# Gated-memory heads: weights in two buffers, differences on ScalarE, products one step behind the weights

## What is computed

```python
D = jnp.where(mask, bh[..., :, None] - bh[..., None, :] + igh[..., None, :], -jnp.inf)
m_t = jnp.maximum(D.max(-1), m_inter)
S = jnp.einsum('bthd,bshd->bhts', qc, kc) * jnp.exp(D - m_t[..., None])
...
h = num / jnp.swapaxes(jnp.maximum(jnp.abs(den), jnp.exp(-m_t)), 1, 2)[..., None]
```

## Time and profile before

| what | value |
|---|---|
| median of three runs | 2977.45 us (2977.14, 2977.45, 2989.36) |
| the profiled execution | 2978.73 us, of which the span from first to last instruction is 2977.0 us |
| gated-memory stage | from about 430 to 545 us of the span |
| PE busy over the span | 2599.6 us (87%) |
| DVE, ACT busy over the span | 848.3 us (28%), 426.1 us (14%) |

### The profile page before, as it was taken

How to read it: one execution, slowest core, us unless ns; L and a number is a source line. 1 busy time by engine, 2 the same in 40 slices (tenths; PEclk the granted TensorE clock), 3 DMA queues, 4 the chain that set the end, 5 groups by cost and what they waited for, 6 DMA issues and landing times.

```text
span 2977.0 us, 34023 instructions
## 1 busy us (share of the span) xinstructions
PE 2599.6 (87%) x13714; PEld 1463.5 (49%) x13714; DVE 848.3 (28%) x1782; ACT 426.1 (14%) x794; POOL 203.2 (7%) x267
## 2 busy tenths in 40 slices
PE   5998986899999997999899888888789988888886
PEld 3454555444444444444486444444377944444443
DVE  3145638510020045300133211111167651111111
ACT  1032211110010013200101100000123411000001
POOL 3122111110010010000010000000000010000000
PEclk8999998899999999999999999999989999999998
DMA  6676578245453543244644599999943066999997
GB/s 243 213 238 245 201 259 286 92 164 168 136 191 132 169 145 99 101 147 159 236 155 146 225 415 420 419 418 420 367 133 99 6 219 243 413 418 420 419 421 303
DMA packets 264855, 721.87 MB, mean 242 GB/s; under 512 B 15248, under 2 KB 149040, under 8 KB 210864
## 3 DMA queue, kind: packets, MB, share of 16 engines
q1 hardware_dynamic: 251232, 690.00, 61.2%
q0 software_dynamic: 13520, 30.41, 3.1%
HBM read 719.17 MB, written 1.18 MB: 242 GB/s over the span
## 4 chain that ended last, share of the span: by engine, by line
PE 67%; DMA 19%; DVE 8%; SPq 2%; issue 2%; ACT 2%; POOL 0%; DVEq 0%; ACTq 0%; POOLq 0%
PE ps L891 23%; DMA ring<-in_moe_w_up 16%; PE ps L1504 9%; PE ps L998 7%; PE ps L916 5%; PE ps L1100 4%; PE ps L1082 2%; SPq L556 2%; DMA ring<-in_ada_w 2%; PE ps L1608 2%; PE ps L1054 2%; PE ps L1494 2%; PE ps L927 1%; PE ps L1444 1%; PE ps L1274 1%
## 5 line engine op out<-in xcount | busy, mean ns | idle before, releaser
L891 PE MATMUL ps<-ring,hT 128*128 128x512 f32 x1632 | 720.6, 596 | 16.6 <-ACT hT L1734 12.5
L891 PEld LDWEIGHTS ps<-ring,hT 128*128 128x128 f32 x1632 | 307.1, 191 | 382.5 <-issue 363.7
L1504 PE MATMUL ps<-arena 128*32 128x512 f32 x1536 | 271.3, 689 | 80.4 <-DMA ring<-in_moe_w_up 71.8
L1504 PE MATMUL ps<-ring,arena 128*32 128x512 f32 x512 | 270.6, 690 | 0.0
L1494 PEld LDWEIGHTS ps<-arena,h 128*128 128x128 f32 x1024 | 248.4, 334 | 17.6 <-issue 14.1
L1494 PE MATMUL ps<-arena,h 128*128 128x128 f32 x1024 | 245.2, 399 | 5.3 <-issue 5.3
L998 PE MATMUL ps<-ring,arena 128*128 128x512 f32 x528 | 232.2, 593 | 2.4 <-ACT arena L1800 2.4
L1504 PEld LDWEIGHTS ps<-arena 128*32 128x32 f32 x1536 | 69.7, 123 | 255.4 <-issue 198.8
L2274 DVE SCALAR_TENSOR_TENSOR arena<-ps,arena 128x256 f32<-128x256 f32 x66 | 28.0, 424 | 578.8 <-ACT arena L1796 578.6
L916 PE MATMUL ps<-hT,ring 128*128 128x256 f32 x768 | 172.3, 387 | 2.5 <-ACT hT L1734 1.5
L998 PEld LDWEIGHTS ps<-ring,arena 128*128 128x128 f32 x528 | 100.1, 190 | 127.7 <-issue 127.7
(11 more groups left out here) (530 smaller groups left out, 2437.8 us busy)
## 6 DMA issues: line engine op xcount, KB each, us to landing
ring<-in_moe_w_down SPq DMA_DIRECT2D x128, 1024.0 KB, 17.7
ring<-in_ada_w SPq DMA_DIRECT2D x48, 2048.0 KB, 12.2
arena<-in_moe_w_gate SPq DMA_DIRECT2D x96, 1024.0 KB, 11.7
arena<-in_moe_w_up SPq DMA_DIRECT2D x96, 1024.0 KB, 9.8
ring<-in_ffn_w_in SPq DMA_DIRECT2D x66, 1024.0 KB, 8.9
ring<-in_ffn_w_out SPq DMA_DIRECT2D x33, 1024.0 KB, 5.0
ring<-in_moe_w_gate SPq DMA_DIRECT2D x32, 1024.0 KB, 15.7
ring<-in_moe_w_up SPq DMA_DIRECT2D x32, 1024.0 KB, 17.8
```

The lines of the kernel that those rows point to most:

```text
L891: m = pe.matmul(o3, lhsT_of(k), ring[:, a:a + 2, k * EH:(k + 1) * EH], start=start and k == 0, stop=stop and k == KC - 1)
L1504: m = pe.matmul(ps[a * CAP:(a + 1) * CAP, 6, :].rearrange("p (u c) -> p u c", u=2), x_slots[:, k, a * CAP:(a + 1) * CAP], slot_pair(gate_s ...
```

## The change

- `p_sb` becomes two buffers, one for each direction.
- The differences move from DVE to ACT: a Relu with scale 1 that reads the row of maxima from `ps`, with -e as bias per partition (the transposed column is copied with scale -1). ACT does the four of a step, then the four exp.
- `seen_by` gives the columns that a key block can be seen from: 512, 384, 256, 128 forwards and 512, 512, 128, 256 backwards, in place of 512, 512, 256, 256. Relu, exp and the product with the scores do only those.
- One masking instruction covers all four diagonal blocks (a strided view, `own_blocks`) in place of four.
- DVE's `weighted(i + 1)` stands in step `i` ahead of the wait for PE's products of step `i`; `weighted(0)` stands before the loop.
- Scores of key blocks 2 and 3 share bank 2; bank 3 is then used for the conditioning groups. PE does the row of maxima two steps ahead, and the next head's scores ahead of the products of an odd step.
- On DVE the order of a step is: (step 0: waits for the values and `out_g`), sums of squares, `ada_rows`, `weighted(i + 1)`, wait for the products, drain.

```diff
-        p_sb = A(4, NT)
+        p_sb = A(2, 4, NT)
...
+        def own_blocks(b):
+            at = p_at + b * 4 * NT
+            return arena[:, at:at + 4 * (NT + P)].rearrange("p (s n) -> p s n", s=4)[:, :, 0:P]
+        def seen_by(si, d):
+            return slice(si * P, NT) if d == 0 else slice(0 if si < 2 else SEQ, NT if si < 2 else (si + 1) * P)
+        def scores_of(si, cols):
+            return ps[:, si, cols] if si < 2 else ps[:, 2, slice(cols.start - SEQ * (3 - si), cols.stop - SEQ * (3 - si))]
...
+            row_max(0)
+            row_max(1)
+            head_scores(0)
+            pe.wait_ge(tp_evacuated, n.tp)
             for hd in range(MLSTM_HEADS):
                 for d in range(2):
                     i = 2 * hd + d
                     pe.wait_ge(sem("ada_rows_ready"), ada_next[0])
-                    if i >= 2:
-                        pe.wait_ge(sem("ml_weights"), 4 * (i - 1))
...
-                    ada_groups(ADA_B[i], 5 - d)
+                    ada_groups(ADA_B[i], 3)
...
-                    pe.wait_ge(sem("ml_weights"), 4 * (i + 1))
+                    pe.wait_ge(sem("ml_weights"), i + 1)
+                    if i + 2 < 2 * MLSTM_HEADS:
+                        row_max(i + 2)
+                    if d == 1 and hd + 1 < MLSTM_HEADS:
+                        head_scores(hd + 1)
                     if i >= 1:
                         pe.wait_ge(sem("ml_out_read"), i)
...
             for i in range(8):
+                act.wait_ge(sem("ml_max"), i + 1)
+                if i >= 2:
+                    act.wait_ge(sem("ml_out"), i - 1)
                 for si in range(4):
-                    k = 4 * i + si
-                    act.wait_ge(sem("ml_gap"), k + 1)
-                    w = p_sb[:, si, (0 if si < 2 else SEQ):NT]
-                    tell(nc.scalar.activation(w, w, ACT.Exp, scale=-1.0), sem("ml_exp"))
+                    nc.scalar.activation(p_sb[:, d, si, seen_by(si, d)], ps[:, 4 + d, seen_by(si, d)], ACT.Relu,
+                                         bias=colsT[:, 0, si, row:row + 1]).then_inc(sem("ml_gap"), 1)
+                for si in range(4):
+                    act.wait_ge(sem("ml_gap"), 4 * i + si + 1)
+                    w = p_sb[:, d, si, seen_by(si, d)]
+                    nc.scalar.activation(w, w, ACT.Exp, scale=-1.0).then_inc(sem("ml_exp"), 1)
...
+            def weighted(i):
+                hd, d = divmod(i, 2)
+                if d == 0:
+                    dve.wait_ge(sem("ml_scores"), hd + 1)
+                for si in range(4):
+                    dve.wait_ge(sem("ml_exp"), 4 * i + si + 1)
+                    w = p_sb[:, d, si, seen_by(si, d)]
+                    V.tensor_tensor(w, w, scores_of(si, seen_by(si, d)), ALU.mult).then_inc(sem("ml_scored"), 1)
+                dve.wait_ge(sem("ml_scored"), 4 * (i + 1))
+                mask = (s_le_t if d == 0 else s_ge_t)[:, :].rearrange("p (o n) -> p o n", o=1).broadcast_to([P, 4, P])
+                V.tensor_tensor(own_blocks(d), own_blocks(d), mask, ALU.mult).then_inc(sem("ml_weights"), 1)
+            weighted(0)
             for hd in range(MLSTM_HEADS):
...
-                    ada_rows(ADA_B[i], 5 - d)
                     if i == 0:
                         dve.wait_ge(sem("ml_v_ready"), 4)
                         dve.wait_ge(sem("out_g_loaded"), 16)
...
                         head_summed(hd - 1)
+                    ada_rows(ADA_B[i], 3)
+                    if i + 1 < 2 * MLSTM_HEADS:
+                        weighted(i + 1)
                     dve.wait_ge(sem("ml_out"), i + 1)
```

More of the change, by code:

```diff
@@ L207, in build @@
         o_ml = A(4, NT)
-        p_sb = A(4, NT)
+        p_at = A.at
+        p_sb = A(2, 4, NT)
         mden = A(3, 4)
@@ L1244, in _, with head_scores, row_max @@
             pe.wait_ge(sem("hg_out_read"), 8)
-            for hd in range(MLSTM_HEADS):
+            def head_scores(hd):
                 q0 = 64 * (hd % 2)
                 qh, kh = qk[q0:q0 + 64, hd // 2, :], qk[q0:q0 + 64, 2 + hd // 2, :]
-                if hd >= 1:
-                    pe.wait_ge(sem("ml_weights"), 8 * hd)
                 for si in range(4):
                     c0 = 0 if si < 2 else SEQ
-                    m = pe.matmul(ps[:, si, c0:NT], kh[:, si * P:(si + 1) * P], qh[:, c0:NT], start=True, stop=True)
+                    m = pe.matmul(scores_of(si, slice(c0, NT)), kh[:, si * P:(si + 1) * P], qh[:, c0:NT], start=True, stop=True)
                 m.then_inc(sem("ml_scores"), 1)
+            def row_max(i):
+                row = 32 * (i % 2) + i // 2
+                pe.matmul(ps[:, 4 + i % 2, :], ident[0:ROWS, row:row + 1].broadcast_to([ROWS, P]), rows_d,
+                          start=True, stop=True).then_inc(sem("ml_max"), 1)
+            row_max(0)
+            row_max(1)
+            head_scores(0)
+            pe.wait_ge(tp_evacuated, n.tp)
+            for hd in range(MLSTM_HEADS):
                 for d in range(2):
@@ L1274, in _ @@
                             m = pe.matmul(ps[:, 6 + ti // 2, (ti % 2) * 129:(ti % 2) * 129 + 129],
-                                          p_sb[:, si, ti * P:(ti + 1) * P], v_tok[:, si, hd, :],
+                                          p_sb[:, d, si, ti * P:(ti + 1) * P], v_tok[:, si, hd, :],
                                           start=si == keys[0], stop=si == keys[-1])
@@ L1943, in _ @@
                 n.tp += 1
-                tell(nc.scalar.copy(colsT[:, i, :, :], src), tp_evacuated)
+                tell(nc.scalar.activation(colsT[:, i, :, :], src, ACT.Copy, scale=-1.0 if i == 0 else 1.0), tp_evacuated)
             for i in range(8):
-                for si in range(4):
-                    k = 4 * i + si
-                    act.wait_ge(sem("ml_gap"), k + 1)
-                    w = p_sb[:, si, (0 if si < 2 else SEQ):NT]
-                    tell(nc.scalar.activation(w, w, ACT.Exp, scale=-1.0), sem("ml_exp"))
+                hd, d = divmod(i, 2)
+                row = 32 * d + hd
+                act.wait_ge(sem("ml_max"), i + 1)
+                if i >= 2:
+                    act.wait_ge(sem("ml_out"), i - 1)
+                for si in range(4):
+                    nc.scalar.activation(p_sb[:, d, si, seen_by(si, d)], ps[:, 4 + d, seen_by(si, d)], ACT.Relu,
[4 more added lines that the diff above has]
+                    nc.scalar.activation(w, w, ACT.Exp, scale=-1.0).then_inc(sem("ml_exp"), 1)
             nc.scalar.preload_act_table(ACT.Sqrt)
@@ L2557, in head_summed @@
                 do(V.tensor_reduce(msum[:, 0, :, 4 + hd], sq4, AX_X, ALU.add))
+            def weighted(i):
+                hd, d = divmod(i, 2)
+                if d == 0:
[8 more added lines that the diff above has]
+            weighted(0)
             for hd in range(MLSTM_HEADS):
-                dve.wait_ge(sem("ml_scores"), hd + 1)
                 for d in range(2):
```

4 lines of the change are left out of this document (removed).

## The result

| | before | after |
|---|---|---|
| median (fewest to most), us | 2978.98 (2977.14 to 2989.36), 4 executions | 2955.38 (2949.84 to 2962.17), 4 executions |
| ratio | | 0.9918, 95% interval 0.99 to 0.9936 |
| profiled execution, us | 2978.73 | 2962.17 |
| its span, us | 2977.0 | 2960.4 |
| end of the last drain in it, us | 540.3 | 512.8 |

23.6 us saved at the medians, where 23 were forecast. The forecast took the 23 off the 2977.45 of three executions; here the kernel before has four, with 2978.98. The profiled execution is the slowest of the four, and its trace shows 16.6 us saved in all, though its gated-memory stage alone saved 27.6.

A forecast was written before the change was run, and what follows sets the result against it. The gated-memory stage was taken as a ring of DVE and PE, ACT having room. Its last drain moving from 540.3 to 517.2 saves 23.1 us, nothing added behind: 2977.45 - 23 = 2954 us, range 2944 to 2966.

The forecast's parts named there:

- Differences on ACT: Gated-memory stage: moving differences takes 17.5 us off DVE; ACT's some 4.2 us a step stays hidden, no table load added.
- Rival 2: ACT becomes late through two table loads a step; saving 13 to 20 us, 2957 to 2964; chance 0.08.
- Product and masks: DVE's product with the scores and one mask per step: 2.6 us, between 2.4 and 2.9, after the change.
- W: Forming a step's weights on DVE: 2.6 us; the prediction is wrong if it takes over 3.5 us.
- Order: Next step's weights form on DVE during PE's products, so one row of work becomes two lines side by side.
- POOL's chain: Group stores and bias loads: 6.3 us a group, starting 6.3 us later at 446.8; DVE waits 4 us in step 4.
- rival 1: POOL's stores and bias loads never bind; drain of step 4 2.9 us earlier, saving 26 us, 2951; chance 0.15.
- The walk: Step-by-step timing of the stage's eight steps: last drain ends at 517.2 instead of 540.3, saving 23.1 us.
- Products: PE's products in each step of the stage: 3.84 us, from 30.7 / 8.
- Rival 3: PE becomes the bound at clock 0.82 and lower; last drain at some 521, saving 19 us, 2958; chance 0.10.
- D(0) to D(7): DVE's drains of PE's products in steps 0 to 7, 2.75 us each; the last forecast to end at 517.2.
- I add and take nothing: Behind the stage: same work in same order, so the stage's 23.1 us saving was carried whole to the end.

The follow-up runs named there:

- dve_diff: Changed kernel with the differences back on DVE, formed a step ahead, ACT doing exp alone: 2961.80 us, ratio 0.9945.
- not_ahead_2: Unaltered repeat of not_ahead, the changed kernel with each step forming its own weights: 2968.57 us, ratio 0.9964.
- store_twice: Changed kernel with each of the stage's 13 group stores done twice, one after the other: 2980.17 us, ratio 1.0001.
- outg_late: Changed kernel with DVE's wait for `out_g` moved from step 0 to step 1: 2956.56 us, ratio 0.9919.
- behind: Changed kernel with outg_late's edit and conditioning groups behind the products on PE and the drain on DVE: 2956.74 us, ratio 0.9937.
- behind_spread: Like behind, with groups per step spread 2, 2, 1, 2, 1, 2, 1, 2: 2956.62 us, ratio 0.992.
- Before_again: The kernel before, unaltered, run once more: 2981.80 us, ratio 1.001.
- not_ahead: Changed kernel with each step forming its own weights on DVE, not a step ahead: 2963.72 us, ratio 0.995.

## Why the prediction held, and where it did not

- **Differences on ACT.** Right, and hidden. The four Relus take 1.78 to 1.89 us (2.0 forecast), four exps 1.55 to 1.67 (2.2 at most). ACT is waited for once, at the head. Undoing it cost 8 us, 6 of them behind the late `out_g` of that trace. For 512 columns ACT took 683 ns where DVE took 748 in dve_diff. Rival 2 fell: the trace has no table load between Relu and exp. By the rule of the Trainium skill ("ScalarE: Activation LUTs", table sets) relu needs no other table; the trace agrees.
- **Product and masks.** W 2.54 against 2.6.
- **Order.** Right in kind. Undone in not_ahead_2 it cost 12 us. Part by part 12 + 8 + 4 = 24, against 26 in all; the parts were each taken out of the full change and needn't add up. Counted from the group ahead of the stage they are 13, 8 and 3.
- **POOL's chain.** The term that failed most. "Store g35 at 446.8" was 445.26, since `out_g` landed at 444.68 and not 446.16, and a group cost (499.14 - 445.26) / 9 = 6.0 us from store to store, not 6.3. The bias of group 44 was there at 486.28 and not 489.5: 1.5 us by the start, 1.2 by six groups from store to store, 0.5 by the load itself. So the 4 us of waiting forecast in step 4 were 0.8, and the wait for a bias until 476.9 forecast in step 3 did not come. The stage ended where rival 1 puts it, but not for its reason: stores did not come near 1.6 us while weights loaded (4.99 each), the chain was only a little earlier than forecast. The bound was near all the same: 0.8 us is not zero, and store_twice shows what is behind it.
- **Groups' weights.** The walk had PE done with group 42 at 473.7; it was 471.38 + 3.19 = 474.57. DVE waited 3.27 us for it and 2.98 for the scores behind it, so that W(4) ended 0.7 us later than forecast, for another reason. With the POOL chain out of the way this is the stage's bound up to step 4; outg_late, behind and behind_spread each ran into these loads or the next in their queue.
- **Products.** 3.84 forecast, 21.0 / 8 = 2.6 measured. This term was mis-sized: the rows of before were the mean of a stretch at 0.82, and the stretch after was at 0.90. Whether closed gaps in PE raised the clock is not shown, since the first 80 us have 0.88 and 0.89. Rival 3, the clock falling, did not come; its 521 is also not the sum of the terms that it gives (446.8 + 43 + 22 is 511.8, or 514.6 with a drain).
- **The walk.** Forecast ends of D(0) to D(7): 452.2, 462.2, 470.5, 484.0, 495.2, 503.5, 510.6, 517.2. Measured: 450.5, 461.2, 468.7, 483.4, 491.9, 500.0, 507.0, 512.8. 2.7 of the 4.4 us at the end came in step 4, and 0.8 in step 7, where products took 2.47.
- **"I add and take nothing" behind the stage.** Off by 11.0 us in the first trace, 2.2 and 9.6 in the other two (last drain against end of span, to the first trace of before). The stage gave 26 at the means and not 23, the medians over all executions 20, and the 23.6 of the first four lies between. So that the time came out within 2 us of the forecast is in part luck: the stage gave more than forecast, the medians kept less of it, and the two errors cancelled. Before_again gives back 3.9 by the same reckoning, and the variants -3.5 to 9.5. So most of what single traces give back is scatter, and whether the change costs later stages anything is not shown.

## What to carry to other kernels

Where two engines take turns, try putting the work of one a step ahead before making it lighter: here the order gave 12 of 26 us without saving any work, the moved work 8 of its 17.5, fewer columns and masks some 4. Price the chain beside the ring, and after it the load that is next in the queue: three attempts at a faster stage ended at the arrival of weights. A forecast made on one stage's end should be held against several executions: behind the stage single traces of the same code differed by up to 14 us, as much as any part of this change is worth.

## What the runs showed of the hardware that was not expected

- The same kernel ran its stage at a granted clock of 0.75 in one execution and 0.89 in another (430 to 510 us of not_ahead and not_ahead_2), with last drains 11.8 us apart. So the program alone does not set the level; what did is not shown.
- In store_twice POOL waited 1.3 to 1.9 us for a 2 KB store to land while no weights loaded and 4.4 to 6.1 while they did, with two such landings 7.5 us apart (482.60 and 490.09).
- The expert rounds, the same code with the same 3943 matmul records in all fourteen traces, took 1046.3 to 1057.1 us, with PE busy 908.1 to 921.4.
- The 512 KB load of `out_g`, issued under the load of weights, took 4.1 to 10.1 us to land in the fourteen traces, 6.4, 7.5 and 5.0 in the three of the changed kernel.
- Relu from `ps` costs ACT 683 ns for 512 columns and 372 for 128, against 643 and 318 for exp within SBUF.
